# Gate and up weights of a mixture-of-experts kernel: two half-megabyte transfers each in place of one of a megabyte

## The reference, cut to what matters

```python
h2 = rmsnorm(x, g_ffn)
...
expert_id = g_idx[..., None] * EXPERTS_PER_GROUP + top_i
combine = jnp.sum(jax.nn.one_hot(expert_id, N_EXPERTS, dtype=jnp.float32) * top_w[..., None], axis=2)
for e in range(N_EXPERTS):
    he = jax.nn.silu(h2 @ w_gate[e]) * (h2 @ w_up[e])
    moe = moe + combine[..., e:e + 1] * (he @ w_down[e]).astype(jnp.float32)
x = x + moe.astype(x.dtype)
```

## Time and profile before

| | |
|---|---|
| median of 3 runs | 432.7 us (432.15 to 432.93) |
| profiled execution, its own time | 431.91 us |
| its span, first to last instruction | 430.1 us |
| TensorE matmuls busy | 411.3 us, 96% of the span |
| VectorE, ScalarE, GpSimd busy | 274.8, 197.8, 127.2 us |
| hardware queue (SP's loads) | 20790 packets, 71.97 MB |
| software queue (POOL's gathers, scatters, stores) | 11248 packets, 18.93 MB |
| expert part, first gate matmul of expert 0 to the last | from 243 us to 419 us |

### The profile page before, as it was taken

The page is one execution under the profiler, slowest core; times in us unless marked ns, Lnnn a source line. Parts: engine busy times, 40 slices in busy tenths (PEclk is TensorE's granted clock), DMA queues, the critical chain, the costliest instruction groups (busy, mean ns, idle before and its releaser), DMA issues.

```text
span 430.1 us, 7803 instructions
## 1 busy us (share of the span) xinstructions
PE 411.3 (96%) x2925; PEld 359.0 (83%) x2925; DVE 274.8 (64%) x663; ACT 197.8 (46%) x486; POOL 127.2 (30%) x210
## 2 busy tenths in 40 slices
PE   7899999999999999999999999999999999998992
PEld 3687999998876876787886899999989999998991
DVE  2856430905759898636457898655566777766984
ACT  5566230704565766332223634444544555554623
POOL 2012000200044324261001414333334555554443
PEclk9999999999999999999999999999999999999996
DMA  8851704506000039933224689999999989987321
GB/s 272 300 190 50 233 2 118 188 2 203 2 1 3 0 120 419 367 145 149 98 99 174 222 329 417 334 412 366 357 354 333 378 329 380 329 335 246 105 87 51
DMA packets 32074, 91.37 MB, mean 212 GB/s; under 512 B 11200, under 2 KB 11712, under 8 KB 27942
## 3 DMA queue, kind: packets, MB, share of 16 engines
q1 hardware_dynamic: 20790, 71.97, 45.2%
q0 software_dynamic: 11248, 18.93, 12.4%
HBM read 86.38 MB, written 26.01 MB: 261 GB/s over the span
## 4 chain that ended last, share of the span: by engine, by line
PE 74%; DMA 12%; DVE 6%; ACT 4%; issue 3%; POOL 0%; SPq 0%; DVEq 0%; ACTq 0%; POOLq 0%
PE ps L1224 18%; PE ps L834 10%; PE ps L836 9%; PE ps L835 9%; DMA region_w<-in_w_down 5%; DMA region_x<-h_rows,lists 5%; PE ps L1264 3%; PE ps L1265 2%; PE ps L1269 2%; PE ps L1217 2%; PE ps L998 2%; PE ps L963 2%; PE ps L1232 2%; DMA region_x<-in_x_prompt 1%; PE ps L981 1%
## 5 line engine op out<-in xcount | busy, mean ns | idle before, releaser
L1224 PEld LDWEIGHTS ps<-region_p,region_a 128*128 128x128 f32 x512 | 58.3, 192 | 1.0 <-DVE region_p L2105 0.4
L1224 PE MATMUL ps<-region_p,region_a 128*128 128x128 f32 x512 | 58.5, 275 | 0.0
L836 PE MATMUL ps<-region_a_r,region_w_r 128*128 128x288 f32 x192 | 56.5, 294 | 0.0
L834 PE MATMUL ps<-region_a_r,ring_r 128*128 128x288 f32 x128 | 40.5, 317 | 0.0
L835 PE MATMUL ps<-region_a_r,ring_r 128*128 128x288 f32 x128 | 37.7, 295 | 0.0
L836 PEld LDWEIGHTS ps<-region_a_r,region_w_r 128*128 128x128 f32 x192 | 36.0, 188 | 0.0
L1639 ACT ACTIVATE region_p<-ps,gffn_sb 128x128 f32<-128x128 f32 x116 | 31.6, 384 | 8.1 <-PE ps L1217 8.1
L1660 ACT ACTIVATE region_t<-ps 128x256 f32<-128x256 f32 x15 | 5.8, 384 | 53.2 <-PE ps L1224 53.2
L707 POOL DMA_INDIRECT region_x<-h_rows,lists x13 | 16.7, 1284 | 45.5 <-DVE slot_w L2208 33.5
L1224 PEld LDWEIGHTS ps<-region_p,ring 128*128 128x128 f32 x256 | 29.1, 192 | 0.8 <-DVE region_p L2127 0.5
L1224 PE MATMUL ps<-region_p,ring 128*128 128x128 f32 x256 | 29.3, 275 | 0.4 <-DVE region_p L2127 0.4
(11 more groups left out here) (381 smaller groups left out, 1030.9 us busy)
## 6 DMA issues: line engine op xcount, KB each, us to landing
region_a<-in_w_gate SPq DMA_DIRECT2D x8, 1024.0 KB, 9.5
region_a<-in_w_up SPq DMA_DIRECT2D x8, 1024.0 KB, 18.5
region_a<-in_w_down SPq DMA_DIRECT2D x8, 1024.0 KB, 18.9
region_w<-in_w_in SPq DMA_DIRECT2D x2, 2048.0 KB, 10.5
region_w<-in_w_out SPq DMA_DIRECT2D x2, 2048.0 KB, 7.9
ring<-in_w_gate SPq DMA_DIRECT2D x4, 1024.0 KB, 8.5
ring<-in_w_up SPq DMA_DIRECT2D x4, 1024.0 KB, 18.0
ring<-in_w_down SPq DMA_DIRECT2D x4, 1024.0 KB, 13.7
```

The lines of the kernel that those rows point to most:

```text
L834: pe.matmul(out, lhs_hi, rhs_hi, start=first, stop=False)
L836: return pe.matmul(out, lhs_lo, rhs_hi, start=False, stop=last)
L1224: ins = pe.matmul(ps[:, 2 + b, (first + c) * P:(first + c + 1) * P], w[:, k, c * P:(c + 1) * P], xT[:, b, k, :], start=(k == 0), stop=(k = ...
```

## The change

`load_gate` and `load_up` each issue two transfers, one for the first four of a partition's eight rows and one for the last four: 128 packets of 4 KB, half a megabyte, in place of 128 of 8 KB. An expert's weights come in five transfers in place of three, and the three waits on their count ask for 80 per round in place of 48. `load_down`, the order of the loads, the ring and all arithmetic stay.

```diff
             def load_gate(slot, e, signal=None):
                 signal = signal or ring_loaded[slot]
-                sp.dma_start(ring[slot][:, 0:WB], wg_v[DS(e, 1)].rearrange("a p n -> (a p) n")).then_inc(signal, 16)
+                for lo in (0, WB // 2):
+                    sp.dma_start(ring[slot][:, lo:lo + WB // 2],
+                                 wg_v[DS(e, 1), :, lo:lo + WB // 2].rearrange("a p n -> (a p) n")).then_inc(signal, 16)
 
             def load_up(slot, e, signal=None):
                 signal = signal or ring_loaded[slot]
-                sp.dma_start(ring[slot][:, WB:2 * WB], wu_v[DS(e, 1)].rearrange("a p n -> (a p) n")).then_inc(signal, 16)
+                for lo in (0, WB // 2):
+                    sp.dma_start(ring[slot][:, WB + lo:WB + lo + WB // 2],
+                                 wu_v[DS(e, 1), :, lo:lo + WB // 2].rearrange("a p n -> (a p) n")).then_inc(signal, 16)
...
-                pe.wait_ge(ring_loaded[u], it * 48 + 48)
+                pe.wait_ge(ring_loaded[u], it * 80 + 80)
...
-                        pe.wait_ge(ov_w_loaded, j * 48 + 48)
+                        pe.wait_ge(ov_w_loaded, j * 80 + 80)
...
-                act.wait_ge(ring_loaded[i % RING], 48 * (i // RING + 1))
+                act.wait_ge(ring_loaded[i % RING], 80 * (i // RING + 1))
```

## The result

**Slower, by 1.3%.** The changed kernel takes 438.22 us (median of 5 runs, 435.54 to 439.12), the kernel before 432.53 beside it (5 runs, 430.69 to 432.93): ratio 1.0128, 95% interval 1.0102 to 1.0155. My forecast was 432.0, "within 0.2%", and its range ended at 435.2.

A forecast was written before the change was run, and what follows sets the result against it. TensorE's own pace bounds the experts, beside 2.0 us of DMA stalls on nearly full engines. 431.91 - 1.26 + 0.6 = 431.25, plus 0.79 from profiled execution to median: 432.0 us, range 430.9 to 435.2.

The forecast's parts named there:

- What bounds the kernel now: Experts, from 230 us: TensorE's own pace, two DMA stalls (0.7 and 1.3 us), 2.0 us winnable; DMA engines nearly full.
- The sign for being wrong altogether: The time moves ahead of 243 us or behind expert 15.
- Part 1, SP's issues: SP's load issues: two more per expert add 0.8 us into 3.0 us of waiting, so they cost nothing.
- Part 2, the price of 4 KB packets: Engines' time for weight loads: smaller packets taken to cost nothing, with 14 us over experts 4 to 14 as upper end.
- slower rival: Experts 7 to 14: weights grow later by a price per expert, deciding over 0.14 us; 434.8 us at 0.25; chance 0.27.
- Part 3, the gathers get ahead: Queues take turns by packet: expert 14's gather stall goes, -1.26 us; expert 7's weights come later, +0.6 us.
- the lag of the experts behind the seventh: Weights of experts 8 and 14 come 0.6 and 1.4 us later, which fits within their room, so no further loss.
- 3.6 us of room: Expert 14's weights: 3.0 us to spare before its gate matmuls, plus 0.6 from the later TensorE.
- Much slower: Weight loads: each transfer's fixed time counts, 2.9 us more per matrix, 46 us over experts 7 to 14, 479; chance 0.03.
- No effect: Queues do not take turns by packet, every landing stays, 432.7 us; chance 0.12.
- Faster: Experts' stalls: gathers win and the weights do not pay, 431.6 us; chance 0.33.

The follow-up runs named there:

- e2: Kernel before, with down's weights loaded in two transfers per expert, all packets kept: 432.07 us, ratio 1.0024.
- e1: Kernel before, with gate and up in 4 KB packets but still one transfer per matrix: 436.32 us, ratio 1.0122.
- e9: Kernel before, plus six 12 MB load blocks behind the last expert: 32.12 and 32.37 us in 8 KB packets, 33.01 in 4 KB, 33.83 in halves.
- e4: Kernel before, with down's weights too in 8 KB packets: 435.42 us, ratio 1.0101.
- e13: The change itself, measured a second time against the kernel before: 437.86 us, ratio 1.0114.
- e8: Kernel before, with the change's half transfers for gate and up of experts 14 and 15 alone: 430.81 us, ratio 0.9959.
- e6: The changed kernel, with down of expert i+3 issued ahead of gate and up of expert i+4: 438.28 us, ratio 1.0131 against the kernel before.

## Why the prediction was wrong

**What bounds the kernel now** was right, and so was its warning: the engines are nearly full, and "what one gets the other lacks". Of the 2.0 us that could be won the 1.3 of the gather's stall were, and 7.8 us were lost beside them. The sign for being wrong altogether did not come: behind expert 15 nothing moved, and ahead of 243 us only 0.5 us.

**Part 1, SP's issues: nothing.** The price held, as far as it was tested: e2, with one issue more per expert and the same packets, is slower by 0.2%, about what a measurement can tell, and e1 loses as much as the change with no issue more. The working did not: an issue doesn't always take 0.4 us, and in the changed kernel two of them held SP for 4.83 us (below). That what they hold back would have stood in the queue anyway is argued; no run separates it.

**Part 2, the price of 4 KB packets: nothing.** Mis-sized: 0.26 us per expert (e9), 2.9 over the 11 experts that I counted. I had compared two stretches of 8 to 10 us with mixed loads, 418 and 416 GB/s; stretches that differ in what else they carry can't show steps of 2.5%. Nor had the first the very shape of the new transfers: it carried 509 packets of 4 KB and 256 of 8 KB, half of its bytes each, the second 256 and 276. The first of them, run again with the change, shows a price: 394 to 411 GB/s in four executions, in place of 418. The slower rival was built on this price, and 0.26 is past the 0.14 that it asked for.

**Part 3, the gathers get ahead.** The direction held, and e1 to e4 fit turns by packet, though no view shows a turn. The step that failed is the lag of the experts behind the seventh: "by the same rule 4 us times 0.071 MB, doubled, is 1.4 us. It fits." Three things in it were wrong.
- *The gain of the gathers.* I scaled the 21.1 us by 0.81 and got 17. It became 8.7. The landings that grow from expert to expert before, and stay level with the change, say that it was mostly a backlog, which grows while a queue gets less than is asked of it and vanishes when it gets a little more. What got ahead of the weights was not 4 us times 0.071 = 0.28 MB, but 0.51 MB, all of it gained between 340 and 394 us.
- *The loss in sum*, 0.39 MB, which part 2 had left out. It came first, by 340 us, ahead of the wait before expert 9. Together the weights were 1.0 MB behind at 394 us (1.23 against 0.24 left).
- *What a megabyte behind is worth.* I turned bytes into time at 418 GB/s, doubled: 4.8 us per MB. Down of expert 14 came 8.8 us later for 1.0 MB (a rough figure: most of the 1.23 MB is down of expert 15, issued at 388.56). The last weights did not flow at the full rate: the engines were busy 0.41 and 0.35 of the time when TensorE waited for them. I had seen that the engines are not alike and put a factor of two on it; the factor was nearly four.

The 3.6 us of room that I gave expert 14 were there, and were spent more than twice over. For expert 7 I had forecast 1.3 us of wait; it was 0.5 in this execution and none in e13's. It was not the expert without room that paid first: which of the early ones did differs between the two executions, and experts 13 and 14 paid in both.

**Rivals.** *Slower, the weights become the bound* is what came: waits at L1228 before several experts and longer landings of w_down, though not the lower rate that it named (357 GB/s from 253 to 394 us in both kernels). Its size, 434.8, was too small by 3.4 us; it had the price without the share. *Much slower* fell: a second transfer in the queue costs 0.068 us per matrix, not 2.9. *No effect* fell with the gather's 8.7 us. *Faster* fell for the whole change and came true for e8, where the weights indeed did not pay.

**Not foreseen at all:** what a wait costs beyond itself, 2.6 of the span's 6.5 us. Four more runs of 64 matmuls begin behind a wait, 0.24 us each: the first can't run beside the product before it and takes 0.35 us in place of 0.27, the others keep their pace. And behind the longest wait the lower clock took 9.01 - 7.38 = 1.63 us.

**Open:** how the loss divides between share, price and clock. From 285 to 394 us the bytes give 0.51 MB to share and 0.39 to price, and by their order in time the waits before experts 7 and 9 would belong to price and the later ones to share; but that is read from bytes, and e1, with no loss in the sum, is as slow as the change within the intervals. Why a few engines end so late isn't shown by these views.

## What to carry to other kernels

In this kernel, with two queues on nearly full DMA engines, the packet size of the one set the share of the other: ask first which of the two has slack, expert by expert, and make the packets small only there (here it paid for the last two experts, and no longer for three). A late transfer on such a queue can be a backlog; don't scale its landing time, but look whether the landings before it grow, count the bytes that change places, and turn them into time by the slow end of the queue, not by its mean rate. A price of 2 to 3% per transfer is measured by blocks of one form from wait to wait, and can't be read from GB/s of mixed stretches.

## What the hardware showed beyond that

**Issues that hold their engine.** SP's timeline of the changed kernel:

```profile
339.17 4.83 SPq L488 DMA_DIRECT2D ring<-in_w_up  x2
344.10 1.64 SPq L493 DMA_DIRECT2D region_w<-in_w_down  x1
```

Before, such an issue took 0.33 to 0.43 us in the earlier trace rows, and 0.93 at most from 285 to 400 us. The last two blocks of e9, where nothing but loads runs, point at the packets that wait in the queue: of twelve loads in 8 KB packets only the last took long, 2.02 us; of twelve in 4 KB packets, one transfer each as well, the eighth already took 2.52. What SP has behind such an issue is held up too.

**Matmuls behind a wait.** Behind waits of 0.3 to 1.7 us for weights the 64 matmuls took 7.38 us in place of 7.14, at a granted clock of 1.00. Behind waits of 2.21 and 2.24 us they took 9.01, at 0.50 to 0.53, and in e4, from 363.6 to 366.9 us, behind its wait of 3.09, the clock was 0.50 as well. But e6's wait of 2.36 us was followed by the ordinary time:

```profile
398.85 7.38 PE L1228 MATMUL ps<-region_p,region_a 128*128 128x128 f32 x64 [2.36 <-DMA region_a<-in_w_down]
```

There the clock stayed at 1.00. So the length of the wait alone doesn't decide it.
